# Gathering the U and V rows of a sparse expert layer apart, and summing the V rows of four tokens on TensorE in 32-column parts

## What is computed

```python
# h: (512, 1024); per token 8 heads x 16 = 128 experts out of 16384
q = (hc @ w_pq).reshape(128, 8, 2, 128)
sc = einsum('thcd,chnd->thcn', q, sub_keys); vals, idx = top_k(sc, 16)
cand = vals[:, :, 0, :, None] + vals[:, :, 1, None, :]
top_s, top_c = top_k(cand.reshape(128, 8, 256), 16)   # experts = the ids of top_c
g = softmax(top_s)
ue, ve = peer_u[experts], peer_v[experts]             # 128 rows of 1024 for each token, twice
act = gelu(einsum('td,thkd->thk', hc, ue))
out = einsum('thk,thkd->td', g * act, ve)
```

## Time and profile before

| | us |
|---|---|
| median of 3 runs (2926.61 to 2928.93) | 2927.49 |
| span of the profiled execution | 2927.4 |
| granted TensorE clock, mean of the span | 0.921 of full speed |
| PE, DVE, ACT, POOL busy | 2491.4, 1760.7, 1133.8, 676.9 |
| moved by DMA | 838.64 MB, 286 GB/s over the span |

### The profile page before, as it was taken

One profiled execution on the slowest core, in us unless ns is written; L12 is line 12 of the kernel. 1 busy time (PEld: TensorE's weight loads), 2 busy tenths in 40 slices (PEclk: granted clock), 3 DMA queues, 4 the chain that ended last, 5 costly groups with the idle time before them and its releaser, 6 DMA issues.

```text
span 2927.4 us, 29566 instructions
## 1 busy us (share of the span) xinstructions
PE 2491.4 (85%) x10118; PEld 1743.2 (60%) x10118; DVE 1760.7 (60%) x4222; ACT 1133.8 (39%) x2762; POOL 676.9 (23%) x566
## 2 busy tenths in 40 slices
PE   8999999879989759888968678588985799988998
PEld 7786666667755437546736544264763376655883
DVE  2101311598797778666989888878998416412430
ACT  2101301242533765354442578464554325512210
POOL 0000000122234343332223445444223101100000
PEclk9999999989989889999989578799997999999999
DMA  5545243689999999999899989999999743432443
GB/s 197 173 154 168 95 144 129 219 335 351 390 394 417 409 397 392 419 389 384 299 332 402 365 301 385 396 420 419 417 418 416 277 159 109 151 130 88 153 155 116
DMA packets 160966, 838.64 MB, mean 286 GB/s; under 512 B 17400, under 2 KB 21896, under 8 KB 95024
## 3 DMA queue, kind: packets, MB, share of 16 engines
q0 software_dynamic: 73728, 536.90, 45.8%
q1 hardware_dynamic: 82464, 287.75, 28.0%
q10 hardware_dynamic: 4624, 12.11, 1.1%
HBM read 828.27 MB, written 8.41 MB: 286 GB/s over the span
## 4 chain that ended last, share of the span: by engine, by line
PE 55%; DVE 18%; ACT 12%; DMA 11%; issue 4%; POOL 0%; ACTq 0%; DVEq 0%; SPq 0%
PE ps L908 26%; DMA BIG<-in_uv,BIG 10%; PE ps L928 5%; PE ps L929 5%; PE ps L1152 5%; DVE BIG L1943 5%; DVE X L1923 4%; PE ps L909 4%; PE ps L1176 2%; PE ps L1177 2%; ACT L1441 2%; DVE BIG L1854 1%; PE ps L1122 1%; DVE BIG L1851 1%; PE ps L1101 1%
## 5 line engine op out<-in xcount | busy, mean ns | idle before, releaser
L2160 POOL DMA_INDIRECT BIG<-in_uv,BIG x512 | 634.2, 1239 | 1646.3 <-DVE BIG L1900 564.6
L908 PE MATMUL ps<-BIG,RING 128*128 128x256 f32 x3472 | 807.6, 385 | 13.8 <-DMA RING<-in_w_cq 4.9
L908 PEld LDWEIGHTS ps<-BIG,RING 128*128 128x128 f32 x3472 | 670.1, 194 | 133.4 <-issue 28.6
L1943 DVE CUSTOM_DVE_ANT_0 BIG<-BIG 128x1024 f32<-128x1024 f32 x512 | 619.6, 1217 | 85.4 <-DMA BIG<-in_uv,BIG 84.2
L1923 DVE SCALAR_TENSOR_TENSOR X<-BIG,small,X 128x1024 f32<-128x1024 f32 x333 | 426.6, 1281 | 91.7 <-ACT small L1445 91.6
L1441 ACT ACTIVATE small<-small 128x1 f32<-128x1 f32 x512 | 102.6, 200 | 620.7 <-DVE small L1943 619.4
L908 PE MATMUL ps<-WK,RING 128*128 128x256 f32 x1232 | 287.2, 385 | 25.2 <-DVE BIG L1702 23.2
L908 PEld LDWEIGHTS ps<-WK,RING 128*128 128x128 f32 x1232 | 235.7, 193 | 65.3 <-DVE BIG L1702 31.1
L928 PE MATMUL ps<-RING,BIG 128*128 128x512 f32 (+1 forms) x448 | 223.0, 579 | 5.0 <-DVE BIG L1681 2.4
L929 PE MATMUL ps<-RING,BIG 128*128 128x512 f32 (+1 forms) x448 | 222.6, 578 | 0.0
L1274 ACT ACTIVATE BIG<-ps 128x256 f32<-128x256 f32 (+2 forms) x143 | 56.8, 398 | 408.5 <-PE ps L909 343.2
(11 more groups left out here) (259 smaller groups left out, 3136.7 us busy)
## 6 DMA issues: line engine op xcount, KB each, us to landing
RING<-in_w_up SPq DMA_DIRECT2D x88, 512.0 KB, 6.0
RING<-in_w_down SPq DMA_DIRECT2D x66, 512.0 KB, 3.6
RING<-in_w_pq SPq DMA_DIRECT2D x32, 512.0 KB, 6.1
RING<-in_w_cc SPq DMA_DIRECT2D x16, 512.0 KB, 8.1
RING<-in_w_cx SPq DMA_DIRECT2D x16, 512.0 KB, 4.1
RING<-in_w_cb SPq DMA_DIRECT2D x16, 512.0 KB, 4.4
RING<-in_w_cv SPq DMA_DIRECT2D x16, 512.0 KB, 5.0
RING<-in_w_gc SPq DMA_DIRECT2D x16, 512.0 KB, 4.7
```

The costliest lines, as they stand in the source:

```text
L908: e.matmul(ps[:, 0:256], W[:, j, :], src[:, j, 0:256], start=j == 0, stop=False)
L1943: e.tensor_tensor_reduce(out=u, in0=HF[:, t % 2, :], in1=u, scale=1.0, scalar=0.0, op0=ALU.mult, op1=ALU.add, accum_out=dots[:, k % 8:k % ...
L2160: e.indirect_dma_start(out=slot[i], out_offset=None, in_=I["uv"], in_offset=bass.IndirectOffsetOnAxis(ap=IDX[:, t, c:c + 1], axis=0)).then ...
```

## The change

U and V are two tensors. A U gather (`urow`, 512 of them) brings the U rows of one expert column for 128 tokens, 512 KB. A V gather (`vrow`, 512 as well) brings the 128 V rows of one token, its experts on the partitions; its index column comes from a transpose of the tile's indices (`turn_ids`, once a tile). There are fifteen slots of 512 KB in place of eight of 1 MB. All dots of a tile are collected, one Gelu on ACT and one product with the gates on DVE serve the tile, and the result is transposed on PE (`turn_gates`). DVE then copies the gates of four tokens (m, 32+m, 64+m, 96+m) into a zeroed strip (`spread`), where each stands alone in a window of 32 columns, and PE multiplies each token's V rows by its window: for each 512-column half four matmuls with 32 columns, each into PSUM partitions 32 j to 32 j + 31 (`vsum`, 128 groups of eight matmuls). `add`, the scaled identities and the DVE sums are gone. `peers` takes U rows and V rows in turn, the V rows of a tile after its U rows, at half the pace a row; a slot is free after its dot (U) or its group's sum (V). `second(0)` starts after `total` of tile 1, and the scores of half 1 lend two slots where they lent one.

```diff
@@ -483,9 +484,10 @@
         def sb(name, shape, dt=F32):
             return ctx.enter_context(nc.sbuf_tensor(name, shape, dt))
 
-        NS = 8
+        NS = 15
         SLOT0 = 3456
-        W0 = SLOT0 + 2048 * NS
+        EXTRA = SLOT0 + 1024 * NS
+        W0 = EXTRA + 1024
         BIG_N = W0 + 16128
         X = sb("X", [128, 4, 1024])
...
+    def take_slot(self, row):
+
+        lent = self.lent_from is not None and (3, 3) not in self.chosen
+        self.turn += 1
+        if self.turn >= (13 if lent else 15):
+            self.turn = 0
+        self.slot_of[row] = self.turn
+        self.slot_before[row] = self.last_in.get(self.turn)
+        self.last_in[self.turn] = row
...
@@ -416,21 +404,12 @@
         yield 0, "kv_in"
         yield from self.cross(1, 1, True)
         self.reached.add("x1")
-        for step in self.experts(1, True):
-            self.light = True
-            yield step
-        for step in self.scores(1, True):
-            self.light = True
-            yield step
-        for step in self.memory():
-            self.light = True
-            yield step
-        while "gain1" not in self.reached or (2, 3) not in self.chosen:
-            self.light = True
+        yield from self.experts(1, True)
+        yield from self.scores(1, True)
+        yield from self.memory()
+        while not self.reached.issuperset(("gain1", ("total", 1))) or (2, 3) not in self.chosen:
             yield "wait"
-        self.light = False
         yield from self.second(0, True)
-        self.light = True
 
     def choices(self):
...
@@ -440,34 +419,56 @@
                 yield from self.choose(t, p, (1.0, 3.0, 1.0, 2.0)[t])
 
     def peers(self):
-        late, n = [], 0
-        for t in range(4):
-            for c in range(128):
-                while (t, c // 32) not in self.chosen:
-                    yield "wait"
-                if t == 2 and c == 0:
+        later, n, u, v, rows_first = [], 0, 0, 0, True
+        summable = set()
+
+        def after(gap, *step):
+            later.append((n + gap, step))
+            later.sort(key=lambda x: x[0])
+
+        while u < 512 or v < 512 or later:
+            while later and later[0][0] <= n:
+                step = later.pop(0)[1]
+                yield (0,) + step
+                self.reached.add(step)
+                if step[0] == "vsum":
+                    self.free.update(("v", step[1], 32 * j + step[2]) for j in range(4))
+            tu, cu = u // 128, u % 128
+            tv, iv = v // 128, v % 128
+            u_ok = u < 512 and (tu, cu // 32) in self.chosen
+            v_ok = v < 512 and tv in summable
+            pace = 1.55 if min(tu, tv) < 2 else 1.25
+            if u_ok and (rows_first or not v_ok):
+                if tu == 2 and cu == 0:
                     yield 1.0, "gain", 1
                     self.reached.add("gain1")
-                k = 128 * t + c
-                self.take_slot(k)
-                yield 0, "expert", t, c
-                for j in late[:]:
-                    if k - j >= (2 if j in self.pe_sums[j // 128] else 1):
-                        late.remove(j)
-                        yield 0, "add", j
-                late.append(k)
-                if not self.norming and (self.light or (1, 3) not in self.chosen):
-                    n += 1
-                    if n % 3 if self.light else n % 2:
-                        self.pe_sums[t].append(k)
-                if c == 1 and t % 2:
-                    yield 0, "total", t - 1
-                yield (3.1 if t < 2 else 2.5), "pace"
-            if t % 2:
-                for k in late:
-                    yield 0, "add", k
-                late = []
-                yield 0, "total", t
+                self.take_slot(("u", tu, cu))
+                yield 0, "urow", tu, cu
+                self.free.add(("u", tu, cu))
+                n, u, rows_first = n + 1, u + 1, False
+                if cu == 104:
+                    after(0, "turn_ids", tu)
+                if cu == 127:
+                    summable.add(tu)
+                    after(2, "gelu", tu)
+                    after(3, "weigh", tu)
+                    after(4, "turn_gates", tu)
+                yield pace, "pace"
+            elif v_ok:
+                m, j = iv // 4, iv % 4
+                self.take_slot(("v", tv, 32 * j + m))
+                yield 0, "vrow", tv, 32 * j + m
+                n, v, rows_first = n + 1, v + 1, True
+                if j == 3:
+                    after(2, "spread", tv, m)
+                    after(3, "vsum", tv, m)
+                if iv == 127:
+                    after(7, "total", tv)
+                yield pace, "pace"
+            elif later:
+                n = later[0][0]
...
@@ -582,10 +584,14 @@
         cf = part(32)
         ids = part(32)
         assert lent[0] <= SLOT0
-        dots = small[:, 480:488]
-        acts = small[:, 488:496]
         ROOM = at_(W0 + 15360, 512)
-        DIAG = [DG[:, 0, :], DG[:, 1, :], at_(W0 + 15872, 128), at_(W0 + 16000, 128)]
+        DOTS = [at_(W0 + 15872, 128), at_(W0 + 16000, 128)]
+        GATES_T, IDS = DG[:, 0, :], DG[:, 1, :]
+        IDX_T = [at_(EXTRA + 544 + 128 * i, 128).bitcast(I32) for i in range(2)]
+        SPREAD = at_(EXTRA, 543)
+
+        def spread_at(t, m):
+            return 128 * ((32 * t + m) % 4) + 31
 
         K0 = W0 + 4096
```

```diff
@@ -1160,21 +1168,33 @@
             def rotate(n):
                 n_banks[0] = n
 
-            def add(k):
-                if k not in pe_turn:
-                    return
-                t = k // 128
-                if pe_turn[k] == 0:
+            def turn_ids(t):
+                ps = bank("ids", t)
+                w.wait_ge(*at["ident"])
+                w.wait_ge(*at["ids", t])
+                e.transpose(ps[:, 0:128], IDS, ident[:, :]).then_inc(pe.sem, pe("mm", "ids", t))
+
+            def turn_gates(t):
+                ps = bank("gates", t)
+                w.wait_ge(*at["weighed", t])
+                e.transpose(ps[:, 0:128], GS[:, t, :], ident[:, :]).then_inc(pe.sem, pe("mm", "gates", t))
+
+            def vsum(t, m):
+                if t == 0 and m == 0:
                     for b in (6, 7):
                         w.wait_ge(*at[("ev",) + held[b]])
                         held[b] = ("experts", b)
-                if k == pe_sums[t][0] and t and pe_sums[t - 1]:
+                if t and m == 0:
                     w.wait_ge(*at["total", t - 1])
-                w.wait_ge(*at["gate", k])
-                v, d = slot[slot_of[k]][:, 1024:2048], DIAG[pe_turn[k] % 4]
-                first, last = k == pe_sums[t][0], k == pe_sums[t][-1]
-                e.matmul(banks[6][:, :], d, v[:, 0:512], start=first, stop=last)
-                e.matmul(banks[7][:, :], d, v[:, 512:1024], start=first, stop=last).then_inc(pacc.sem, pacc("sum", k))
+                w.wait_ge(*at["spread", t, m])
+                for j in range(4):
+                    w.wait_ge(*at["slot", "v", t, 32 * j + m])
+                for hh in range(2):
+                    for j in range(4):
+                        d = spread_at(t, m) + 32 * j - m
+                        v = slot[slot_of["v", t, 32 * j + m]][:, hh * 512:(hh + 1) * 512]
+                        mm = e.matmul(banks[6 + hh][32 * j:32 * j + 32, :], SPREAD[:, d:d + 32], v, start=m == 0, stop=m == 31)
+                mm.then_inc(vsums.sem, vsums("vsum", t, m))
 
             def prepare():
...
+            def gelu(t):
+                w.wait_ge(*at["dot", t, 127])
+                e.activation(DOTS[t % 2], DOTS[t % 2], ACT.Gelu).then_inc(act.sem, act("gelu", t))
 
             def final_in(tag, h):
                 for name in final_start(tag, h):
...
-                if k // 128 == 0:
-                    w.wait_ge(*at["ev", "co", 0, 1, 1])
-                elif k // 128 == 2:
-                    w.wait_ge(*at["ev", "co", 1, 1, 1])
-                w.wait_ge(*at["gate", k])
-                w.wait_ge(acc.sem, acc.n)
-                e.scalar_tensor_tensor(out=X[:, t, :], in0=slot[slot_of[k]][:, 1024:2048], scalar=acts[:, k % 8:k % 8 + 1],
-                                       in1=X[:, t, :], op0=ALU.mult, op1=ALU.add).then_inc(acc.sem, acc("sum", k))
-
             def total(t):
-                w.wait_ge(*at["sum", 128 * t + 127])
-                w.wait_ge(acc.sem, acc.n)
-                if pe_sums[t]:
-                    w.wait_ge(*at["sum", pe_sums[t][-1]])
-                    for hh in range(2):
-                        d = X[:, t, hh * 512:(hh + 1) * 512]
-                        e.tensor_tensor(d, banks[6 + hh][:, :], d, ALU.add).then_inc(dve.sem, dve("total", t))
-                        at["ev", "experts", 6 + hh] = (dve.sem, dve.n)
-                else:
-                    at["total", t] = (acc.sem, acc.n)
-
-            def expert(t, c):
-                k = 128 * t + c
-                u = slot[slot_of[k]][:, 0:1024]
+                w.wait_ge(*at["ev", "co", t // 2, 1, 1])
```

(89 more changed lines are left out.)

83 lines of the change are left out of this document (23 added, 60 removed).

## The result

After: 3066.7 us, median of 4 runs (3063.19 to 3070.91). Before, run beside it: 2928.21 (2926.61 to 2932.33). The ratio is 1.0476, 95% interval [1.046, 1.0492]: slower by 138 us. The forecast was +30, 2957 us, with a range of 2870 to 3090. The profiled execution took 3070.91 us, its span is 3069.0.

What follows compares the result with a forecast made beforehand. DMA was taken to bound most of the gather middle, PE its beginning, DVE its third quarter. Middle 1678 + 116 - 37 + 20 = 1777 against 1747, +30: 2957 us; own range 2915 to 3000, stated range 2870 to 3090.

Steps and rivals of the forecast that it cites:

- Slots and waits: Alternating U and V stretches: 3.5 MB ahead instead of 6 MB fits on average; charged +20 us, ends 0 and +160.
- the sign that shows it: In V-with-U stretches, DVE's dots would wait for gathers while POOL waits for `vsum`.
- 79 cycles: Cycles of eight rows in the planner's order, charged 0.25 us each, +20; at 2 us each, +160.
- The budget of 9.1 us in 11.5: Dot, copy, PE chunk, group, gather issue and latency take 9.1 us; seven rows ahead at 1.6 us give 11.5.
- POOL as the bound: Rival, every stretch with dots: gathers held by dots make POOL need 1833 us, total 3013; chance 0.15.
- POOL: 1024 gathers for 512, about 1475 us or 1.44 a row; just slower than DMA in the attentions, nothing charged.
- 4 KB rows: Gathers in the middle: 537 MB in 4 KB rows at q1's price, +47 us, floor becomes 1678.
- Reliefs: 559 to 907 and 1400 to 1864 us: less PE and DVE work gives back a third of 111 us, -37.
- PE: Adds go (307 us), 128 groups of eight matmuls come at about 1.9 us, 250 taken: -57 us of PE work.
- the parts don't overlap: Rival, PE groups: four parts run one after another, 6.9 us a group, total at least 3145, about 3200; chance 0.15.
- What starts later: `second(0)` starts at row 577 instead of 514; only a tail of two chunks, +3 us, inside the rounding.
- The fast rival: Middle: gaps came from adds and table loads, short lookahead holds, DMA full throughout; total 2890, chance 0.28.

Runs made afterwards that it cites:

- e4: The changed kernel with each V slot free once its row has landed, group matmuls reading a constant tile, so V rows aren't summed: 2915.83 us, ratio 0.9959.
- e5: The changed kernel with eleven slots in use instead of fifteen (nine while two are lent): 3493.59 us, ratio 1.1952.
- e14: The kernel before, with a second gather of 64 bytes to each of 8 partitions behind each of its own: 2980.23 us, ratio 1.0192.
- e1: The kernel before, each pair gathered by two DMAs of 512 KB (4 KB rows) into its old slot: 2983.89 us, ratio 1.0187.
- e10: The changed kernel with early strip copy and rows in runs of four (e3 again, another set): 2994.48 us, ratio 1.0243.
- e11: As e10, on the same chip, with tile 1's V rows ahead of tile 2's U rows: 2992.63 us, ratio 1.024.
- e3: The changed kernel with the strip copy at the group's first V row and rows in runs of four (UUUU VVVV): 2954.36 us, ratio 1.0095.
- e12: The kernel before, with a second gather of 64 bytes to all 128 partitions behind each of its own: 2995.34 us, ratio 1.0247.

## Why the prediction was wrong

**Slots and waits: this step failed.** The prediction named the right mechanism and the sign that shows it, and mis-sized the term. Its 79 cycles at 0.25 us gave +20, with +160 as the far end. e4 puts the hold at 151 us, 1.9 us a cycle. All the other terms together came to -12 us in e4, where the sum had +10. The budget of 9.1 us in 11.5 was made of typical durations taken one by one. The turn at 1958 to 1975 us shows what it lacked. The sum took 3.64 us, not 1.9. It stood behind a whole attention step that itself waited 6 us for DVE, not behind half a chunk. And the terms feed each other: a late row delays the softmax, which delays the sum, which delays the next rows. A delay is carried on rather than taken up. Every one of the 79 cycles was taken as independent and as fitting "on average". Nor did the seven rows ahead hold throughout: while two slots are lent, thirteen are in turn and five rows are ahead. By the order of `take_slot` that is so from the 434th to the 571st gather, 1363 to 1645 us in after. No run tests the lending alone; e5 shows how steep the slope is.

That the stated range holds 3067 is in part luck. The far end of this term, +160, would reach it, but the forecast's own range ended at 3000. The only other case between that and 3090 was POOL as the bound (3013), and under **POOL** below it is shown false.

**4 KB rows.** Charged at 2.50 us a MB. In e4, with the DMA engines full (share 1.01), q0 took 0.825 x 361 / 117.20 = 2.54 against 2.41. At that price the gathers would need 537 x 0.128 = 69 us more of the DMA engines, an estimate. But not all of it is the row size. e14 keeps the 8 KB rows, and its q0 in the same stage took 0.807 x 361 / 117.57 = 2.48:

```profile
q0 software_dynamic: 19707, 117.57, 80.7%
```

So about half of the rise comes with the doubled gathers, and the +47 for the rows alone is not refuted. Nor do e1 and e14, +56 each, show the rows as a time of their own in the order of before.

**Reliefs.** Charged at -37. In e4 the total is 12 us under before. If the 69 us above were paid in full, 81 us came back; no run parts the two. The stage 559 to 907 us gave almost none of it (373 GB/s in e4, 371 before), the stage 1400 to 1651 most (390 for 344). In after itself nothing came back in either, nor from 1651 to 1864 us: 371, 344 and 361 GB/s became 366, 316 and 353. Freed DVE and PE time is worth nothing while rows are not there.

**PE.** A group takes 1.92 us with nothing in its way, as taken, so the rival that the parts don't overlap falls: one after another they would need 6.9. At the clock they met, the 128 took 325.7 us, 2.54 each, where 250 was charged. The Trainium skill (TensorE: Matmul & The Clock Gate, Part 3) gives three column parts a speedup of 2.38; the estimate for four from that was 2.2 us. Here eight matmuls of 0.86 us in 1.92 are a speedup of 3.6 for four, and the measurement decides.

**POOL.** The mean gather was 1.12 us, as foreseen (1.15), and e4 hides all 1024 beside DMA, so the rival of POOL as the bound falls: it made 3013, and POOL had waits of 366 us for sums. But the charge of nothing for doubled gathers does not hold everywhere. In the order of before a second gather costs 56 us even when it brings only 64 bytes to 8 partitions (e14). The forecast had no term for that, and how much of it after pays is not shown.

**What starts later.** Three us for `second(0)` fits: e10 and e11 differ by 2.

**The fast rival** (2890) had 0.28. e4 is as near as it gets, at 2916, without the sums' hold. In after the middle ends at 2447 us, 1888 us long, over the 1820 at which the forecast called itself wrong.

## What to carry to other kernels

When a change replaces a buffer that one consumer frees by one that several rows must free together, count the bytes ahead at the moment of release in the stage with the least other traffic. Follow the wait around all engines until it comes back to its start. Here the worst duration a cycle, 2 us, gave 160 and the runs 151, while the mean gave 20. Engine time that is freed beside a full transfer queue is worth nothing if the same edit shortens what that queue has ahead. Before splitting the transfers, look at the small helper that releases them (here a copy of 0.15 us) and at the order of the rows: the copy ahead of what can wait for a transfer, and rows that leave together coming together, were worth 100 us on one chip.

## What the runs showed that I had not expected

Kernels with little ahead differ from set to set where the kernel before doesn't. After took 3066.7 and 3094.39 us, e3's kernel 2954.36, 2994.48 and 2996.82 on three chips, while the medians of before lie between 2923.31 and 2928.21. Whether it is the chip or something else of the set isn't shown, since no chip on record ran two sets.

An indirect gather's time on POOL hardly depends on how much it brings. The medians are 877 ns for 64 bytes to 8 partitions (e14), 952 for 64 bytes to 128 (e12), 948 for 4 KB to 128 (after) and 947 for 8 KB to 128 (before). The means, 1059 to 1239 ns, are longer by the gathers that meet a dot: in after the median of the 355 that start during one is 1.36 us, and they end 0.82 us after it.
